# A search cut up between matrix products: the orders of four engines ahead of and behind the gate chunks of a hybrid layer

## What is computed

```python
(u_a, z_a, q, k, v, z_b, q_idx, k_idx, w_idx, g_a, g_b) = jnp.split(proj, split_points, axis=-1)
y_a = multiscale_pool(u_a, w_pool_group, pool_scale) * jax.nn.silu(z_a)
score = jnp.einsum('bqhs,bqh->bqs', relu(q_idx . k_idx), w_idx)     # causal
_, idx = lax.top_k(score, 256)                                      # then attention over these keys
y_b = attn * jax.nn.silu(z_b)
merged = sigmoid(g_a) * (y_a @ w_branch_a) + sigmoid(g_b) * (y_b @ w_branch_b)
x = x + gate * (merged @ w_out)
```

## Time and profile before

| | us |
|---|---|
| median of 3 runs | 859.35 (858.17 to 861.89) |
| profiled execution | 860.57 |
| its span | 858.8 |
| PE busy | 790.9 |
| VectorE busy | 588.1 |
| ScalarE busy | 476.4 |
| GpSimd busy | 406.0 |

### The profile page before, as it was taken

How to read it: one execution, slowest core, us unless ns; L and a number is a source line. 1 busy time by engine, 2 the same in 40 slices (tenths; PEclk the granted TensorE clock), 3 DMA queues, 4 the chain that set the end, 5 groups by cost and what they waited for, 6 DMA issues and landing times.

```text
span 858.8 us, 13053 instructions
## 1 busy us (share of the span) xinstructions
PE 790.9 (92%) x4318; PEld 667.5 (78%) x4323; DVE 588.1 (68%) x1207; ACT 476.4 (55%) x890; POOL 406.0 (47%) x375
## 2 busy tenths in 40 slices
PE   6999999989966878789999789699999999999998
PEld 4988988878855666568888567478888888888987
DVE  5876787897975777668777966436666896772522
ACT  5664456752336957658898523388777884330100
POOL 1102523154534694578776733666788931540000
PEclk9899999999998997999999989999999999999999
DMA  9930200033432021433433304564242303654331
GB/s 347 366 98 1 81 31 13 1 100 114 137 116 77 22 86 50 134 109 112 134 106 106 122 32 136 201 221 140 95 147 87 99 1 121 211 197 153 117 104 57
DMA packets 65649, 98.43 MB, mean 115 GB/s; under 512 B 6153, under 2 KB 37165, under 8 KB 65582
## 3 DMA queue, kind: packets, MB, share of 16 engines
q1 hardware_dynamic: 55970, 78.70, 28.7%
q10 hardware_dynamic: 7692, 12.60, 3.9%
q0 software_dynamic: 1920, 6.29, 1.8%
HBM read 71.36 MB, written 26.21 MB: 114 GB/s over the span
## 4 chain that ended last, share of the span: by engine, by line
PE 63%; DVE 15%; ACT 9%; issue 4%; DVEq 3%; DMA 3%; ACTq 1%; POOL 1%; POOLq 1%; SPq 1%
PE pp L879 12%; PE pp L880 11%; PE pp L881 11%; ACT ps L1695 4%; PE pp L1371 3%; PE pt L1346 3%; DVE score L2469 2%; PE ps L1120 2%; PE ps L1119 2%; PE ps L879 2%; PE ps L881 2%; PE ps L880 2%; DVE junk L2494 1%; DVE cand L2513 1%; DMA scale_w<-in_w_ada 1%
## 5 line engine op out<-in xcount | busy, mean ns | idle before, releaser
L879 PE MATMUL pp<-hT_hi,w_hi 128*128 128x512 f32 x212 | 87.8, 414 | 27.6 <-ACT ua L1657 16.9
L1695 ACT ACTIVATE ps<-score,cand 128x896 f32<-128x896 f32 (+3 forms) x96 | 96.6, 1006 | 23.4 <-DVE cand L2513 8.0
L880 PE MATMUL pp<-hT_lo,w_hi 128*128 128x512 f32 x212 | 86.0, 405 | 0.0
L881 PE MATMUL pp<-hT_hi,w_lo 128*128 128x512 f32 x212 | 85.7, 404 | 0.0
L2682 DVE TENSOR_TENSOR pT<-pt,pT 128x512 fp32r<-128x512 f32 (+3 forms) x96 | 50.5, 554 | 45.1 <-ACT pT L1903 42.0
L879 PEld LDWEIGHTS pp<-hT_hi,w_hi 128*128 128x128 f32 x212 | 42.1, 199 | 41.1 <-issue 17.7
L2494 DVE TENSOR_SCALAR_CACHE_REDUCE junk<-score,cand 128x384 uint8<-128x384 f32 (+3 forms) x94 | 68.3, 752 | 4.2 <-issue 0.5
L879 PE MATMUL pp<-w_hi,hT_hi 128*128 128x256 f32 (+1 forms) x208 | 69.0, 332 | 1.8 <-POOL w_lo L819 1.1
L880 PE MATMUL pp<-w_lo,hT_hi 128*128 128x256 f32 (+1 forms) x208 | 67.5, 324 | 0.0
L881 PE MATMUL pp<-w_hi,hT_lo 128*128 128x256 f32 (+1 forms) x208 | 67.4, 324 | 0.0
L819 POOL TENSOR_TENSOR w_lo<-w_raw,w_hi 128x1024 fp32r<-128x1024 f32 x23 | 58.7, 2563 | 16.7 <-ACT w_hi L814 15.5
(11 more groups left out here) (388 smaller groups left out, 2320.3 us busy)
## 6 DMA issues: line engine op xcount, KB each, us to landing
w_raw<-in_w_in SPq DMA_DIRECT2D x36, 512.0 KB, 3.7
sgb_spill<-stage SPq DMA_DIRECT2D x16, 256.0 KB, 2.3
sga_spill<-stage SPq DMA_DIRECT2D x16, 256.0 KB, 2.1
stage<-sga_spill SPq DMA_DIRECT2D x16, 256.0 KB, 3.5
ma_spill<-stage POOLq DMA_DIRECT2D x16, 256.0 KB, 2.4
gate_w<-in_w_ada SPq DMA_DIRECT2D x16, 256.0 KB, 2.8
w_raw<-in_w_out SPq DMA_DIRECT2D x8, 512.0 KB, 4.1
e_in<-sgb_spill SPq DMA_DIRECT2D x16, 256.0 KB, 3.1
```

The lines of the kernel that those rows point to most:

```text
L879: nc.tensor.matmul(o, a_hi, b_hi, start=first, stop=False)
L880: nc.tensor.matmul(o, a_hi, b_lo, start=False, stop=False)
L881: return nc.tensor.matmul(o, a_lo, b_hi, start=False, stop=last)
L1695: last = nc.scalar.activation(ps[1][:, 0:keys(b)], score[:, score_at(b):score_at(b + 1)], ACT.Sign, scale=-1.0, bias=cand[:, n:n + 1].bitc ...
```

## The change

Pass numbers and places move; the work stays the same except for where the sums of tile 2 are done.

- 14 passes (0 to 13) stand ahead of the gate chunks instead of 16. Pass 0 goes on ScalarE between the last three zb tiles, in two halves. Pass 14 goes into chunk 0 after product 4, passes 15 to 29 stand where 16 to 30 stood, pass 30 at the head of chunk 6.
- `sums(2)` goes from VectorE to GpSimd, ahead of the window means, with `late_b` for its temporaries and a semaphore `sum_2_ready`; `pooled_round(1)`, which writes where they lay, waits until they are stored.
- The copies of units, the sums and the stores are put in another order on ScalarE and VectorE ahead of the chunks; za unit 6 now stands before the first four gate blocks, and `first_part(0)` waits for four low sums instead of six.
- All eight chunks use four banks; uses of `ps` carry a bank of their own (`ps_bank`), the tie counts always `ps[1]`.
- `search_end` is cut in three (`search_end`, `search_check`, `search_take`), and the masks move: 2 and 3 begin in chunk 6, all else happens in chunk 7 (the eighth) and behind it.

```diff
-    MASK_T = {43: 2, 44: 3, 49: 4, 50: 5, 55: 6, 56: 7}
-    MASK_C = {45: (2, 3), 50: (4,), 52: (5,), 56: (6,), 57: (7,)}
+    MASK_T = {49: 2, 50: 3, 52: 4, 53: 5, 55: 6, 56: 7}
+    MASK_C = {50: (2,), 51: (3,), 53: (4,), 54: (5,), 56: (6,), 57: (7,)}
...
-        pp_bank += [(PRODUCTS * chunk + j) % (4 if chunk < G_WIDE else 2) for j in range(PRODUCTS)]
+        pp_bank += [(PRODUCTS * chunk + j) % 4 for j in range(PRODUCTS)]
...
+    ps_bank = [n % 2 for n in range(len(ps_uses))]
     ps_uses += [(("cum", b), "v") for bs in MASK_C.values() for b in bs]
+    ps_bank += [1] * NSEL
     ps_uses += [(("S", i), "v") for i in range(HEADS)]
+    ps_bank += [i % 2 for i in range(HEADS)]
...
-        G_COUNTS, G_SEARCH = {}, {}
+        G_SEARCH = {(0, 4): 14, (6, 0): 30}
         for n in range(15):
-            G_SEARCH[1 + n // 3, 2 * (n % 3)] = G_COUNTS[1 + n // 3, 2 * (n % 3)] = [16 + n]
+            G_SEARCH[1 + n // 3, 2 * (n % 3)] = 15 + n
...
              for n in range(len(ZB_ORDER)):
                 zb_tile(n)
+                if n == len(ZB_ORDER) - 3:
+                    counts(0, 4, 6)
+                if n == len(ZB_ORDER) - 2:
+                    counts(0, 6)
...
+            def sums(k):
+                t0, t1, t2, t3 = sum_temps(k)
+                f0, f1 = slice(0, HALF), slice(HALF, L)
+                gp.tensor_tensor(t0, hT_hi[:, k, f1].bitcast(F32), hT_lo[:, k, f1].bitcast(F32), ALU.add)
+                gp.tensor_tensor(t1, hT_hi[:, 4 + k, f1].bitcast(F32), hT_lo[:, 4 + k, f1].bitcast(F32), ALU.add)
+                gp.tensor_tensor(t2, hT_hi[:, k, f0].bitcast(F32), hT_lo[:, k, f0].bitcast(F32), ALU.add)
+                gp.tensor_tensor(t3, hT_hi[:, 4 + k, f0].bitcast(F32), hT_lo[:, 4 + k, f0].bitcast(F32), ALU.add)
+                pool.drain()
...
+            sums(2)
             window_mean(0)
+            split_chunk_lo(pool, name_of[("za", 0)])
             pooled_low(0)
-            split_chunk_lo(pool, name_of[("za", 0)])
```

More of the change, by code:

```diff
@@ L571, in sum_temps @@
         def sum_temps(k):
-            two = k % 2
-            first = sum_a if two == 0 else sum_b
-            return first[:, 0, :], first[:, 1, :], first[:, 2, :], z_silu[:, two, :]
+            if k == 2:
+                return tuple(late_b[:, i, :] for i in range(4))
+            first = sum_a if k == 0 else sum_b
+            return first[:, 0, :], first[:, 1, :], first[:, 2, :], z_silu[:, k % 2, :]
         V_POS, V_SIN, V_MEAN, V_RSQRT = 1, 2, 3, 4
@@ L1357, in _ @@
                     o = ps_claim(("S", i))
+                    if i == 0:
+                        for j in range(3, PRODUCTS):
+                            wait_done(pe, pp_done[pp_at[("g", NG - 1, j)]], pp_free_a, pp_free_v)
                     two_pass(o, qT[:, b % 2, h, :], kT, keys(b)).then_inc(ps_full, 1)
@@ L1634, in _, with counts @@
                             split_chunk_hi(act, name_of[("q", i)] + 2)
+            def counts(k, first=None, last=NT):
+                act.wait_ge(cand_ready, k + 1)
+                for b in range(COUNT_FROM[k] if first is None else first, last):
+                    n = b - FREE_BLOCKS
+                    act.drain()
+                    done = nc.scalar.activation(ps[1][:, 0:keys(b)], score[:, score_at(b):score_at(b + 1)], ACT.Sign, scale=-1.0,
+                                                bias=cand[:, n:n + 1].bitcast(F32), accum_out=cnt_a[:, n:n + 1])
+                if last == NT:
+                    done.then_inc(counted, 1)
             for n in range(len(ZB_ORDER)):
                 zb_tile(n)
+                if n == len(ZB_ORDER) - 3:
+                    counts(0, 4, 6)
+                if n == len(ZB_ORDER) - 2:
+                    counts(0, 6)
                 if n == 3:
@@ L1686, in sum_high @@
                 nc.scalar.activation(sum_home(l)[0], raw, ACT.Copy).then_inc(s_hi, 1)
-            def counts(k):
-                a = COUNT_FROM[k]
-                act.wait_ge(cand_ready, k + 1)
-                for b in range(a, NT):
-                    n = b - FREE_BLOCKS
-                    act.drain()
-                    last = nc.scalar.activation(ps[1][:, 0:keys(b)], score[:, score_at(b):score_at(b + 1)], ACT.Sign, scale=-1.0,
-                                                bias=cand[:, n:n + 1].bitcast(F32), accum_out=cnt_a[:, n:n + 1])
-                last.then_inc(counted, 1)
             def block_hi(q):
@@ L2618, in _ @@
             sums(0)
+            search(0)
             sums(1)
             sum_2_low(0)
-            search(0)
-            sums(2)
+            search(1)
             sum_2_low(1)
-            search(1)
+            search(2)
+            sum_2_low(2)
+            search(3)
             sums(3)
-            sum_2_low(2)
+            search(4)
             sum_2_low(3)
-            for k in range(2, 10):
+            for k in range(5, 9):
                 search(k)
@@ L2727, in _ @@
                         sum_low(l)
+                if c == NG - 2:
+                    search_end()
                 if c == NG - 1:
-                    mask_end(4)
+                    mask_end(2)
+                    mask_begin(4)
                 middle(c, 2)
-                for k in G_SEARCH.get((c, 2), ()):
-                    search(k)
+                if (c, 2) in G_SEARCH:
+                    search(G_SEARCH[c, 2])
+                if c == NG - 2:
+                    search_check()
+                if c == NG - 1:
+                    mask_end(3)
+                    mask_begin(5)
                 middle(c, 3)
```

147 lines of the change are left out of this document (74 added, 73 removed).

## The result

The changed kernel took 829.74 us (median of 4 runs, 828.4 to 834.25) against 860.14 for the kernel before; the ratio is 0.9656 with a 95% interval of 0.9613 to 0.970. The forecast was 827. The profiled execution took 828.40 us, its span is 826.3.

The account below looks back on a forecast made before the run. PE was busy 790.9 of 858.8 us, so its waits at the two ends could be won back. Gains 20.4 + 0 + 12.3 = 32.7 took the profiled 860.57 to 827.9, 827 against the median; range 811 to 845.

Parts of the forecast that it names:

- Stretch ahead: From the first ua unit to gate product 0: fewer PE waits under the new order, gain 20.4 us.
- The floor of 95.4: Ahead of the gate chunks: 132.4 us less 30.2 of waits and 6.8 of clock drops leaves 95.4.
- The 2 us for held candidates: Ahead of the chunks: a third of 13 passes' candidate instructions held, mostly hidden behind ScalarE's copies; 2 us added.
- Pass 0, costed at nothing: On ScalarE among the last zb tiles: about 1 us delay, covered by 4 us of spare bank claims, so cost nothing.
- Passes 14 and 15: On ScalarE right before the copies of za units 6 and 7: 2 x 3.45 = 6.9 us, all on the path.
- Sums of tile 2: Ahead of the chunks: GpSimd's eight adds take 13 us, ready at 250.5; candidate 2 at 250 instead of 262.00.
- Chunks 0 to 5: Gate chunks: chunk 0 keeps its length, pass 14's lag fits in four banks; cost 0, bounds 0 and 5.
- Chunk 6 to branch A: Product 42 to the fourth branch-A unit: 59.8 of work plus 7.7 of waits, 67.5 instead of 79.8; gain 12.3 us.
- C: Rival, the two ends: half of the 21 us of remaining waits gone too; gain 43 to 48, 814 us; chance 0.17.
- B: Rival, ahead of the chunks: most candidates held by the shared port, 17 us lost; gain 17, 842 us; chance 0.13.
- D: Rival, ahead of the chunks: GpSimd's window means become the chain, only the 12 behind stay; 847 us; chance 0.05.
- E: Rival, gate chunks: VectorE and ScalarE bound them, PE waits 2.2 us in each of 17 passes; 864 us; chance 0.05.

Follow-up runs that it names:

- the reordering of chunk 0: Changed kernel with sums 3 cut, tie order and loads moved, plus ScalarE's high parts of sums 8 to 11 ahead of chunk 0's weight blocks: 818.94 us.
- the cut alone: Changed kernel with VectorE's sums 3 cut in two around pass 4's decision and their store behind the copy of ua 6: 825.57 us.
- the further edits: Changed kernel plus sums 3 cut in two, tie transposes, copies and counts reordered, SP loads earlier, and chunk 0's high parts ahead of weight blocks: 818.94 us.
- ties moved: Changed kernel with tie copy 6 ahead of the last two ya rows and mask 7's transposes and counts each one branch-A unit later: 829.94 us.
- ties and loads moved: Changed kernel with the new tie order, and SP's second q row and fourth gate tile loaded ahead of the wait for all biases: 827.51 us.
- the kernel of 823.54 us: Changed kernel with sums 3 cut in two, the new tie order and the earlier SP loads together, sums 1 in one piece: 823.54 us.
- the one with sums 3 cut as well: Changed kernel with sums 2 on VectorE again and sums 3 cut in two around pass 4: 827.23 us.
- the back part alone: Kernel before with only four banks in all chunks, the search end cut in three and masks in the eighth chunk: 850.56 us.

## Why the prediction was right, and where its steps were not

The time was right within 3 us and the mechanism is the one forecast. But three terms were off (+4.4, -2.2, -4.3), and that their sum is only 2.1 is in part luck.

**Stretch ahead, 20.4 forecast, 24.8 measured.** Right in kind: the waits for ua and za fell from 25.9 to 9.3 ("about 11"). The walk's marks, on the clock of before: unit 4 forecast at 255.3, came at 254.2; za 0 at 284.4, came at 283.7; product 0 at 340.8, came at 336.5. The four waits 4.6 + 0.7 + 5.0 + 2.9 measured 3.42, 0, 5.85 and 1.08. *The floor of 95.4 was too high*: it came from before's length less waits and drops at 1.7 each; after's 107.7 us less 10.4 of waits and 4.3 of slow clock leave 93.0, where the count had 92.7. *The 2 us for held candidates* were not on the path. Of the 14 that follow passes 0 to 13, 8 took 0.86 to 2.32 us instead of 0.23, some 10 us more in all, so not "a third" but more than half were held; yet from za 0 to product 0 PE had the one wait of 1.08.

**Pass 0, costed at nothing:** right, and its worth (8.1 us by the run without it) was inside the walk, as said. **Passes 14 and 15, 6.9 all on the path:** on the path, yes, but the 6.9 is only near: with them back product 0 comes 3.2 later, product 1 10.1 and product 42 6.3.

**Sums of tile 2.** The durations were right: GpSimd's adds 1.74 while VectorE adds too (forecast 1.75), all eight 13.1 us (13), done at 250.4 on the clock of before (250.5). Their first and last rows in after, and the end of sums 3 on VectorE beside GpSimd's split:

```profile
235.09 1.74 POOL L2131 TENSOR_TENSOR late_b<-hT_hi,hT_lo 128x512 f32<-128x512 f32 x1
...
246.93 1.30 POOL L2141 TENSOR_TENSOR late_b<-late_b 128x512 f32<-128x512 f32 x1 [0.15 <-issue]
```
```profile
257.60 2.92 DVE L2595 TENSOR_TENSOR sum_b<-hT_hi,hT_lo 128x512 f32<-128x512 f32 x1
...
271.55 1.37 DVE L2604 TENSOR_TENSOR z_silu<-z_silu,sum_b 128x512 f32<-128x512 f32 x1
```

But the step compared candidate 2 at 250 with the 262.00 of before and left it there, as if the move had brought it. The same rows price the other place: eight free adds are 8 x 0.69 = 5.5 us, five stretched ones 5 x 1.05 = 5.2. The runs with the sums on VectorE show a draw. What brought the candidate forward was pass 0, by the run with it behind the zb tiles, and for the rest the new order, which no run isolates. Sums 3 took 15.9 us (256.99 to 272.92) where the walk had 14.7 (261.3 to 276), and as a block in front of one decision they were the cause of the 5.85.

**Chunks 0 to 5, cost 0 forecast (bounds 0 and 5), 2.2 measured.** The step that failed is "chunk 0 keeps its length": it looked at the loads' distance only. Product 7 came 26.7 us after product 0 instead of 25.5, and product 9 waited 0.8. The loads are not all that sets the chunk's length. GpSimd's second weight part was begun 13.2 us ahead of product 0 before, and is begun 0.2 ahead of it now:

```profile
334.09 1.75 POOL L2090 TENSOR_TENSOR w_lo<-w_sum,w_hi 128x512 fp32r<-128x512 f32 x1
```

ScalarE's high parts of h stand behind its weight sums; the reordering of chunk 0 gave 3.8 us between products 0 and 7 (27.4 to 23.5; 3.1 against the 26.6 of the cut alone, which has the same chunk 0). The cover of 1.3 us for pass 14 was enough: chunks 2 to 5 took 19.04 us each, and of the 110 us from 338 PE was busy 104.39 (106.09 in the earlier trace rows).

**Chunk 6 to branch A, 12.3 forecast, 8.0 measured.** The wait for the first tie mask went, as forecast, and the tie copy stood behind ya_in (1.92; forecast 2.5). Two terms were mis-sized. For the masks of chunk 7 the forecast had "another 2 in all", where mask 7 alone was waited for 3.73 us. And no clock drop was counted behind the waits, though two were taken off for before; 2.4 us were lost there. 59.8 + 9.4 + 2.4 = 71.6, for 71.9 measured (457.3 to 529.2; forecast 67.5). Ahead of mask 7 VectorE's comparison, which took 0.75 us in the kernel before, was held by GpSimd's weight split (508.55 to 510.89):

```profile
508.94 2.50 DVE L2689 TENSOR_SCALAR eq<-score,thr 128x1024 bf16<-128x1024 f32 x1
```

That hold doesn't explain the wait, though: in three kernels with the same order there, where the comparison took 1.27 or 1.28 us (sums 3 cut, sums 2 on VectorE, pass 0 behind zb), PE waited for mask 7 3.36 to 3.50. Pass 30 in chunk 6 costs 2.1 to 2.6 of the stretch, by the runs without it; the forecast had that in its waits for product 49 and the sums 46 to 48 (3.2 together), of which 1.36 came.

**Rivals.** C, fewer waits (814), was not reached by the change; the further edits, which take away or shorten the waits of 5.85, 2.96, 3.73 and 1.92, come to 818.94. B, the port decides ahead (842): its condition came true, most candidates are held, but its price did not, as they are held behind PE's work. D is refuted by product 0, which moved 24.8. E is refuted: PE has no wait from product 10 to product 49.

## What to carry to other kernels

When work moves to another engine, price the same work in the best place on the old one too; the gain of an order is easily credited to the move. Count a clock drop with every wait of the size that was followed by one in the trace (here every one of 2.9 us and more; 1.72 was not; in between, the same wait was in one kernel and not in another), at the end of a walk as at its start. And when a stage is reached earlier, list everything that used to be ready long before it, on the slow engines and in the load queue: each such distance has shrunk, and the next bound is the shortest of them.

## What was not expected of the hardware

- The same wait of 2.9 to 3.0 us for product 6 cost different amounts of slow clock. In after the 4 us from 354 are at 0.62 and the next four at 0.95. With the ties moved, with ties and loads moved and with sums 2 on VectorE two windows are low (0.58 and 0.57 in the last); in the kernel of 823.54 us three are (0.56, 0.50, 0.66). Of PE's own rows, what the matmuls there took above their 0.227 us each comes to 1.4 us in after, 2.2 to 2.6 in the three, and 3.7 in the last. The wait of 2.75 for the unit behind ua 2 tells the same: the 4 us behind it have 0.50 in the kernel with sums 2 on VectorE and 1.00 in the one with sums 3 cut as well, and the code up to there is the same. So do the kernel before, with 0.57 behind a wait of 2.80, and the back part alone, with 1.00 behind the same wait (2.83).

```profile
260.00:264.00 4.00, 4.00 (x11) 3.14 (x10) 4.00 (x3) 3.85 (x6) 4.00 (x2) 0.50 0.07 9
```
```profile
260.00:264.00 4.00, 4.00 (x19) 3.26 (x19) 4.00 (x3) 3.85 (x6) 4.00 (x2) 1.00 0.05 7
```

Why is open, as the code ahead of the wait is the same in each pair.

- Instructions on VectorE that read one tile are held beside GpSimd as well: the comparison of 128x1024 above took 2.50, and 0.75 in the kernel before; the acceptance of 128x3 values 0.17 and 1.63. The counting form with an accumulator was not: 1.28 for 128x1024 beside GpSimd too. The Trainium skill (SBUF - State Buffer, "Who interferes with whom") names instructions with two SBUF inputs and those in a two-port mode as the ones that take part, and says that tensor_scalar can enter such a mode, but not in the form that also writes out its accumulator. The rows above agree, as the comparison and the acceptance are TENSOR_SCALAR; that they ran in that mode no trace here shows, and the prediction counted only instructions with two inputs.
- The unchanged first part of the kernel ended anywhere in a range of 5.8 us over the profiled executions, more than most of the edits here are worth. The aligned traces take that out, but keep the spread of 1 to 2 us told above; for less than that neither decides.
